# Taking the filler matmuls out of TensorE's waits in a five-block transformer kernel

## What is computed

```python
for i in range(4):                       # first_block
    kind = i % 3                         # 0 retention, 1 gated recurrence (RG-LRU), 2 latent attention (MLA)
    h = layer_norm(ALPHA * h + mix, ln_g[i, 0], ln_b[i, 0])
    h = layer_norm(ALPHA * h + sq_relu_mlp(h, mlp_w1[i], mlp_w2[i]), ln_g[i, 1], ln_b[i, 1])
...
x = x + 0.5 * swiglu(rmsnorm(x, ffn1_norm), ...)          # second_block
x = x + hybrid_mixer(rmsnorm(x, mix_norm), ...)           # dilated attention and grouped-query attention
x = x + 0.5 * swiglu(rmsnorm(x, ffn2_norm), ...)
return rmsnorm(x, final_norm)
```

## Time and profile before

| what | us |
|---|---|
| median of 3 runs | 2188.84 |
| lowest and highest of them | 2186.75, 2191.39 |
| the profiled execution's own time | 2182.95 |
| its span, first to last instruction | 2181.1 |

### The profile page before, as it was taken

The page is one execution under the profiler, slowest core; times in us unless marked ns, Lnnn a source line. Parts: engine busy times, 40 slices in busy tenths (PEclk is TensorE's granted clock), DMA queues, the critical chain, the costliest instruction groups (busy, mean ns, idle before and its releaser), DMA issues.

```text
span 2181.1 us, 29320 instructions
## 1 busy us (share of the span) xinstructions
PE 2067.2 (95%) x12304; PEld 1796.5 (82%) x12304; DVE 1327.2 (61%) x1297; ACT 924.2 (42%) x862; POOL 79.5 (4%) x52
## 2 busy tenths in 40 slices
PE   8999999979999879999999999989989999799998
PEld 7988888877888757887988888879978878698997
DVE  6766756688666646667656666664454556464444
ACT  5344333375333433333345433343343446444333
POOL 0000000100000100001000000010010000001000
PEclk9999999989999999999999999999999999999999
DMA  8443555434554504554535355525446553243552
GB/s 314 155 161 148 212 192 190 162 116 155 203 194 156 178 11 170 194 188 161 209 149 188 134 208 192 193 95 204 192 154 218 156 148 116 78 157 128 201 198 96
DMA packets 32362, 364.17 MB, mean 167 GB/s; under 512 B 3677, under 2 KB 3938, under 8 KB 10130
## 3 DMA queue, kind: packets, MB, share of 16 engines
q1 hardware_dynamic: 28146, 347.49, 43.2%
q0 software_dynamic: 4128, 15.39, 2.8%
HBM read 361.77 MB, written 1.10 MB: 166 GB/s over the span
## 4 chain that ended last, share of the span: by engine, by line
PE 82%; DVE 11%; ACT 4%; DMA 2%; issue 1%; SPq 0%; DVEq 0%; ACTq 0%
PE acc L863 26%; PE bank L823 9%; PE bank L825 9%; PE bank L824 9%; PE bank L1300 8%; PE bank L1302 4%; PE bank L850 3%; PE bank L852 2%; PE bank L851 2%; DVE h L2222 2%; DVE w_lo L2139 1%; DVE w_lo L2134 1%; DMA raw<-slabs_in 1%; ACT w_hi L1581 1%; PE bank L1428 1%
## 5 line engine op out<-in xcount | busy, mean ns | idle before, releaser
L823 PE MATMUL bank<-ht_both,w_hi 128*128 128x256 f32 x1696 | 476.7, 281 | 2.2 <-DVE ob_lo L2737 1.9
L825 PE MATMUL bank<-ht_both,w_lo 128*128 128x256 f32 x1696 | 473.9, 279 | 0.0
L824 PE MATMUL bank<-ht_both,w_hi 128*128 128x256 f32 x1696 | 473.6, 279 | 0.0
L2139 DVE TENSOR_TENSOR w_lo<-raw,w_hi 128x4096 fp32r<-128x4096 f32 (+4 forms) x83 | 310.3, 3738 | 127.2 <-ACT w_hi L1581 127.1
L1569 ACT ACTIVATE w_hi<-raw 128x2048 fp32r<-128x2048 f32 x166 | 308.6, 1908 | 143.5 <-PE bank L825 138.6
L1581 ACT ACTIVATE w_hi<-raw 128x4096 fp32r<-128x4096 f32 (+4 forms) x91 | 283.6, 3116 | 188.7 <-PE bank L1302 156.6
L2134 DVE TENSOR_TENSOR w_lo<-raw,w_hi 128x2048 fp32r<-128x2048 f32 x114 | 256.2, 2288 | 118.4 <-ACT w_hi L1569 118.4
L823 PEld LDWEIGHTS bank<-ht_both,w_hi 128*128 128x128 f32 x1696 | 318.3, 188 | 7.7 <-issue 6.6
L824 PEld LDWEIGHTS bank<-ht_both,w_hi 128*128 128x128 f32 x1696 | 318.3, 188 | 1.6 <-issue 0.5
L825 PEld LDWEIGHTS bank<-ht_both,w_lo 128*128 128x128 f32 x1696 | 318.5, 188 | 0.0
L1300 PE MATMUL bank<-ht_both,w_hi 128*128 128x512 f32 x768 | 269.1, 393 | 0.0
(11 more groups left out here) (339 smaller groups left out, 3094.8 us busy)
## 6 DMA issues: line engine op xcount, KB each, us to landing
raw<-slabs_in SPq DMA_DIRECT2D x147, 2048.0 KB, 7.7
raw<-slabs_in SPq DMA_DIRECT2D x23, 1024.0 KB, 6.3
raw<-slabs_in SPq DMA_DIRECT2D x12, 512.0 KB, 9.6
g_tab<-gains_in POOLq DMA_DIRECT2D x11, 512.0 KB, 4.9
a_bias<-bias_rows POOLq DMA_DIRECT2D x8, 576.0 KB, 7.0
b_tab<-gains_in POOLq DMA_DIRECT2D x8, 512.0 KB, 5.9
raw<-slabs_in SPq DMA_DIRECT2D x2, 1152.0 KB, 5.8
raw<-slabs_in SPq DMA_DIRECT2D x1, 1280.0 KB, 5.7
```

The lines of the kernel that those rows point to most:

```text
L823: nc.tensor.matmul(o, whi, xhi, start=first, stop=False)
L824: nc.tensor.matmul(o, whi, xlo, start=False, stop=False)
L825: return nc.tensor.matmul(o, wlo, xhi, start=False, stop=last)
L2139: nc.vector.tensor_tensor(w_lo[slot][:, 0:w], raw[slot][:, 0:w], w_hi[slot][:, 0:w].bitcast(F32), ALU.subtract).then_inc(lo_ready, 1)
```

## The change

The helper `keep_clock` is taken out with all its calls. Where it stood, the wait for the bank that it began with stays, so the order of all other instructions and all other waits is as before.

```diff
-            def keep_clock(key, count):
-                wait_free(*key)
-                for _ in range(count):
-                    nc.tensor.matmul(psum(*key)[:, :], ident, cst[:, 0:512], start=True, stop=True)
...
                 if ahead is not None:
                     ahead()
-                    transposes(n, 1, keep=False)
+                    transposes(n, 1)
                     return
-                keep_clock(("tr", TR_AFTER[n], 1, 0), 8 if n == N_LN else 3)
+                wait_free("tr", TR_AFTER[n], 1, 0)
                 transposes(n, 1)
...
                 for half in range(2):
                     key = ("tr", tr, t, half)
-                    if n is not None and t == 1 and half == 1 and keep:
-                        keep_clock(key, 1)
-                    else:
-                        wait_free(*key)
+                    wait_free(*key)
...
                 def second_blocks():
-                    keep_clock(rest, 2)
+                    wait_free(*rest)
                     blocks_ready(1)
-                keep_clock(rest, 2)
+                wait_free(*rest)
                 blocks_ready(0)
...
                     key = ("mt", hd)
-                    if hd >= 4:
-                        keep_clock(key, 2)
-                    else:
-                        wait_free(*key)
+                    wait_free(*key)
                     pe.wait_ge(m_prob, hd + 1)
```

More of the change, by code:

```diff
@@ L917, in down_end, with transposes @@
                     ahead()
-                    transposes(n, 1, keep=False)
+                    transposes(n, 1)
                     return
-                keep_clock(("tr", TR_AFTER[n], 1, 0), 8 if n == N_LN else 3)
+                wait_free("tr", TR_AFTER[n], 1, 0)
                 transposes(n, 1)
-            def transposes(n, t, keep=True):
+            def transposes(n, t):
                 source = h if n is None or n < N_LN else hn
```

## The result

Eight runs of the kernel without fillers have a median of 2196.82 us (2195.29 to 2200.66), eight of the kernel before 2188.75 us (2182.52 to 2191.39). The ratio is 1.0042, with a 95% interval of 1.0030 to 1.0054, or +9.2 us (+6.6 to +11.8). The forecast was slower, by 5.3 us to 2194.1 us; the time lies inside the forecast range, but nearer to rival (d) at 2198.8.

A forecast was written before the change was run, and what follows sets the result against it. The prediction took TensorE, the VectorE steps it waits for and its clock as the bound. Path -1.7, norms 1, 3, 5 +3.3, heads +3.4 and LRU +0.3 made +5.3 us on the 2188.84 median: 2194.1 us, range 2187.0 to 2200.0.

The forecast's parts named there:

- rival (d): Transposes raise the clock poorly, so norms 8 to 10 pay 4.5 us on top: about +10, 2198.8 us; chance 0.22.
- Rival (b): Only a long unbroken pause lowers the clock, so only the gain on the path remains: -1.7, 2187.1 us; chance 0.22.
- Rival (c): Fillers run at the low clock and delay norms 1, 3 and 5 by up to 1.5 us each; removal gives 2182; chance 0.06.
- the one for norms 8 to 10: Norms 8 to 10: first products start sooner, -1.2 us for the three, with no added clock cost.
- it stays low for several stretches behind the norms 8 to 10 (d): Sign of being wrong: in the profile after, the clock stays low for several stretches behind norms 8 to 10.
- terms for norms 1, 3 and 5: One clock fall at each of the three norms without fillers: +3.3 us together (0 to +9.6).
- the heads: MLA heads 4 to 7: two more low stretches at 1.6 us each, reaching into the down products; +3.4 us (0 to +6).
- The part on the path: Time regained from fillers that delay work, at norms 8 to 10, norm 3 and head 4: about -1.7 us (0 to -2.9).
- the 0.7 us at norm 9: Norm 9: without the second-half filler the next block's first product can start 0.75 us sooner.
- the 0.15 us from VectorE to the first product: Norms 8 to 10, profile after: the first product follows VectorE's L2168 within 0.15 us.
- no loss in the LRU block: LRU block: a fall before the second products in fewer than half of the executions; +0.3 us (0 to +0.8).
- the 40 to 48 of the fillers: Profile after: TensorE's busy time falls by 40 to 48 us, from 82 records of 0.59 us, overlapping a little.

The follow-up runs named there:

- e1: Kernel before with fillers taken out only at the ends of norms 1, 3 and 5; median 2191.07 us, ratio 1.0009.
- e3: Kernel before with fillers taken out only at norms 8, 9 and 10; median 2189.14 us, ratio 1.0010.
- e2: Kernel before with fillers taken out only in MLA heads 4 to 7; median 2193.35 us, ratio 1.0029.
- e6: Kernel before with longer fills before tile 1 at norms 8 to 10 and added fillers in tile 0 at norms 1, 3, 5; 2174.37 us, ratio 0.9943.
- e7: Kernel of e6 with fillers in three more pauses (LRU blocks 2 and 4, hybrid mixer); 2172.15 us, 0.9927 of the kernel before.
- e4: Kernel before with each filler matmul replaced by eight 128-column transposes of the constants; median 2189.13 us, ratio 1.0010.
- e12: Kernel of e7 with every filler matmul replaced by eight transposes, timed beside e10; 2174.39 us, 0.9942 of the kernel before.
- e5: Kernel before without the single filler before the second half of tile 1 at norms 8, 9 and 10; 2190.29 us, ratio 1.0003.
- e10: Kernel of e7 unchanged, run again on another chip; 2173.43 us, 0.9938 of the kernel before.

## Why the prediction was right, and where it was wrong

**The direction and the mechanism were right.** The clock falls more often, and that is where the time goes. e1 to e3 put it at the places named (e2 by time, the other two by their profiles and clocks), e6 and e7 show it from the other side: more fillers, a higher clock, less time. Rival (b), only long pauses, is refuted by e2. Rival (c), slow fillers on the path at norms 1, 3 and 5, would have made e1 faster by up to 4.5 us; its interval allows a gain of 0.7 at most.

**The failed step is the one for norms 8 to 10**: "no cost beyond the part above, if the transposes and the earlier products raise the clock again as soon as before". They didn't: the clock came up 2.9 to 4.0 us behind the first product, where before and in e2 it had come up within 0.7 (in e1 too, but for 2.5 at norm 10). That "it stays low for several stretches behind the norms 8 to 10 (d)" was one of the prediction's own signs of being wrong, and it came in part. The term was -1.2 us, and the trace after gives +1.5 (0.7, 0.6, 0.2), e3 by time +2.2 (-0.2 to +4.6). I drew it from one row, 13 transposes in 1863.00 to 1866.40 with 2.76 us busy, after which the clock rose. In the trace after, the same transposes, busy for slightly less of the stretch, were followed by another low one:

```profile
1873.90:1877.30 3.40, 2.49 (x13) 2.11 (x11) 0.00 (x0) 2.61 (x5) 0.00 (x0) 0.50 0.00 0
```

So the row was a close case and no proof that the stretch at norm 9, 2.50 us busy, would do. Rival (d) had the longer low time at these norms, but neither its size (4.5 us on top, measured 2.7 by trace) nor its cause: it isn't that they are transposes (e4, e12), it is that TensorE idled where the filler had been. The filler that looked like pure cost, 1.71 us on the path at norm 9, had kept it busy between the two groups; e5, which takes out only that one, keeps the clock low at least as long as e3 does.

**The terms for norms 1, 3 and 5 and for the heads** had the right sign and were too small in the trace: 6.2 for 3.3 - 0.35 = 2.95, and 4.1 for 3.15. At the norms, I counted one new stretch after the pause. The traces have two or more at the low clock there, which also slow the transposes, and at norm 1 of the trace after reach back over the last products of tile 0. For the heads, e2 measured 6.3 us by time (4.2 to 8.7), at the far end of the bound of 6, and 4.2 by record: two heads have their scores in a low stretch, and the tail reaches into the down products. By time the norms are less certain: 2.0 us in e1 (-0.7 to +4.8), so their term may as well have been too large. The two errors that stand out lie on one side (the late norms too low by 2.7 us by trace, the heads by 1 to 3), so the whole came out 3.9 us above the forecast; it stayed inside the range because that reaches up to rival (d). The part on the path was also added up wrongly: -1.2 - 0.35 - 0.25 is -1.8, not -1.7.

**The part that came out to the letter** is the small one: the 0.7 us at norm 9, the 0.15 us from VectorE to the first product, and no loss in the LRU block (forecast +0.3). TensorE's busy time fell by 21.7 us (2067.2 - 2045.5) and not by the 40 to 48 of the fillers, since products at the low clock are busy for longer. The clock ended at 0.972, under the 0.976 I gave.

## What to carry to other kernels

A filler in a wait is to be priced by the clock at which the work behind it runs, not by whether it overruns the wait: at norm 9 one that cost 0.7 us on the path returned at least about as much. Where a filler is to hold the clock, let it last until just before the data come: 18 passes in place of 6 at norm 9 and the like elsewhere made this kernel 0.6 to 0.7% faster than before, and it is the version to keep (e7). Lengths in between were not run. Before such an edit is judged by a single pair of traces, look at what the places without an edit do: here they moved by up to 2.6 us each.

## What the runs showed of the hardware

- The clock fell behind stretches whose longest pause was 2.04 us (802.10 to 805.50, 1.13 us busy of 3.40). A long unbroken pause isn't needed (e2: +6.3 us, +4.2 to +8.7).
- Equal busy times did not mean the same at the two levels. At the full clock, a stretch with 2.43 us busy of 3.40 was followed by the full clock (e10, 1630.80). At the low clock, stretches with 2.50 and 2.75 us busy were followed by another low one (after, 1645.20; e5, 1640.70). The records at the low clock last longer, so the same work looks busier there.
- Transposes held the clock as matmuls did (e4 at 406.30; e12's 0.993 against e10's 0.994), and helped to raise it at the norms 8, 9 and 10 of e4.
- The same kernel's low stretches lie elsewhere in each execution, and a place without an edit moved by up to about 2.6 us.
- Eight executions of the kernel before spread over 8.9 us, six of e7's over 3.0 (2170.00 to 2173.02). Fewer falls are not enough to explain it: eight executions of the kernel after, with the lowest clock of all, spread over 5.4 us.
